# Head norms: sums on four 32-column groups, and factors spread by one fp32r matmul per head from a rounded row and a remainder row

## What is computed

```python
def rms_norm(x, g):
    y = xf * lax.rsqrt(jnp.mean(xf * xf, axis=-1, keepdims=True) + EPS)
    return (y * g).astype(x.dtype)

h = rms_norm(from_chunks(h), norm_g.reshape(ML_HEADS, ML_DH))   # 4 heads of 192
o = rms_norm(from_chunks(o), norm_g.reshape(HG_HEADS, HG_DV))   # 6 heads of 128
qd = rms_norm_2(q_d.reshape(B, S, DIL_HEADS, DIL_DIM), g_q_dil) # 8 heads of 128
kd = rms_norm_2(k_d.reshape(B, S, DIL_HEADS, DIL_DIM), g_k_dil)
q_nope, k_nope = rms_norm_2(q_nope, g_q_nope), rms_norm_2(k_nope, g_k_nope)
```

## Time and profile before

| | us |
|---|---|
| median of 3 runs | 2983.12 (2980.38 to 2985.36) |
| span of the profiled execution | 2978.0 |
| PE busy | 2946.2 (99%) |
| DVE busy | 2051.0 (69%) |
| ACT busy | 1311.7 (44%) |
| DMA | 50.7% of 16 engines, 178 GB/s |

### The profile page before, as it was taken

The page is one execution under the profiler, slowest core; times in us unless marked ns, Lnnn a source line. Parts: engine busy times, 40 slices in busy tenths (PEclk is TensorE's granted clock), DMA queues, the critical chain, the costliest instruction groups (busy, mean ns, idle before and its releaser), DMA issues.

```text
span 2978.0 us, 47097 instructions
## 1 busy us (share of the span) xinstructions
PE 2946.2 (99%) x18616; PEld 2630.0 (88%) x18616; DVE 2051.0 (69%) x2624; ACT 1311.7 (44%) x1418; POOL 70.0 (2%) x72
## 2 busy tenths in 40 slices
PE   8999999999999999999999999999999999999999
PEld 8898898999988888888888888876998888888888
DVE  6675787977788888885557776636666666666444
ACT  5354423444444444444444354425445444444333
POOL 0000000000001000000000000000000000000000
PEclk9999999999999999999999999999999999999999
DMA  6553334555555555555555544531555555555555
GB/s 230 184 183 134 114 120 149 168 173 198 186 196 193 189 196 194 190 182 190 193 195 198 195 172 168 186 122 43 184 198 186 195 197 188 193 197 177 194 193 184
DMA packets 87359, 530.39 MB, mean 178 GB/s; under 512 B 9952, under 2 KB 10336, under 8 KB 41184
## 3 DMA queue, kind: packets, MB, share of 16 engines
q1 hardware_dynamic: 87264, 529.07, 50.7%
HBM read 526.94 MB, written 2.10 MB: 178 GB/s over the span
## 4 chain that ended last, share of the span: by engine, by line
PE 96%; DVE 2%; ACT 1%; DMA 0%; issue 0%; SPq 0%; DVEq 0%; ACTq 0%
PE bank L576 74%; PE late L576 22%; DVE arena L1687 1%; DVE w_low L1687 0%; DVE half_low L1687 0%; DVE arena L1684 0%; ACT w_high L1203 0%; PE late L1144 0%; DVE arena L1989 0%; DMA ring<-in_w_gates 0%; DMA xT<-in_xT 0%; DVE acts_both L1687 0%; DVE arena L2045 0%; DVE arena L2016 0%; DVE xrs L1734 0%
## 5 line engine op out<-in xcount | busy, mean ns | idle before, releaser
L1687 DVE TENSOR_TENSOR w_low<-ring,w_high 128x2048 fp32r<-128x2048 f32 (+1 forms) x480 | 1014.3, 2113 | 384.1 <-ACT w_high L1203 380.2
L1203 ACT ACTIVATE w_high<-ring 128x2048 fp32r<-128x2048 f32 (+1 forms) x480 | 849.5, 1771 | 636.0 <-DMA ring<-in_w_down 223.0
L576 PE MATMUL bank<-up_early,w_high 128*128 128x512 f32 x1408 | 487.8, 389 | 0.0
L576 PE MATMUL bank<-up_late,w_high 128*128 128x512 f32 x1408 | 487.3, 389 | 0.0
L576 PE MATMUL late<-acts_both,w_high 128*128 128x512 f32 x1408 | 479.0, 389 | 0.3 <-DVE w_low L1687 0.3
L576 PE MATMUL bank<-up_early,w_low 128*128 128x256 f32 x1408 | 388.6, 276 | 0.0
L576 PE MATMUL late<-acts_both,w_low 128*128 128x256 f32 x1408 | 388.6, 276 | 0.0
L576 PE MATMUL bank<-up_late,w_low 128*128 128x256 f32 x1408 | 388.6, 276 | 0.0
L576 PEld LDWEIGHTS bank<-up_early,w_high 128*128 128x128 f32 x1408 | 264.5, 188 | 55.2
L576 PEld LDWEIGHTS late<-acts_both,w_high 128*128 128x128 f32 x1408 | 264.3, 188 | 55.1 <-DVE w_low L1687 0.6
L576 PEld LDWEIGHTS bank<-up_late,w_high 128*128 128x128 f32 x1408 | 264.0, 188 | 54.7
(11 more groups left out here) (311 smaller groups left out, 4946.2 us busy)
## 6 DMA issues: line engine op xcount, KB each, us to landing
ring<-in_w_up SPq DMA_DIRECT2D x176, 1024.0 KB, 4.7
ring<-in_w_down SPq DMA_DIRECT2D x128, 704.0 KB, 4.0
ring<-in_w_in SPq DMA_DIRECT2D x66, 1024.0 KB, 4.7
ring<-in_w_mix SPq DMA_DIRECT2D x62, 1024.0 KB, 4.8
ring<-in_w_gates SPq DMA_DIRECT2D x96, 512.0 KB, 3.7
ring<-in_w_branch SPq DMA_DIRECT2D x16, 1024.0 KB, 4.7
ring<-in_w_out SPq DMA_DIRECT2D x16, 1024.0 KB, 4.8
ring<-in_w_o SPq DMA_DIRECT2D x16, 1024.0 KB, 4.8
```

Source lines behind the costliest of these rows:

```text
L576: return nc.tensor.matmul(o, lhsT, rhs, start=first, stop=last)
L1203: A(w_high[:, s, 0:cols], ring[:, s, 0:cols], ACT.Copy).then_inc(rounded[s], 1)
L1687: return V.tensor_tensor(o, a, b, op)
```

## The change

It alters the two matmul steps of a head norm and the DVE step between them. No matmul is added or removed.

- **Sums.** `pick` windows are 32 columns wide instead of 8, and head h goes to output partitions 32*(h%4) on, so four heads in a row use four different 32-column groups of the array. The order is piece by piece, heads inside. The ones stand twice in a window, so that a head's sum lies in row 32*(h%4) + h//4 and again 16 rows lower.
- **Factors.** DVE works on all 128 partitions. Its last step becomes three: the product rounded to fp32r into `rows_r`, the exact product into `xms`, and `rows_r * sign + xms`, where `sign` is 0 in the upper 16 rows of a group and -1 in the lower 16. The upper rows so hold the rounded factor, the lower the remainder.
- **Spread.** The stationary operand is a column of `row_sel` (fp32r) with ones in the two rows of a head; it and `rows_r` are fp32r, so each matmul adds rounded factor and remainder in one pass.
- **Set-up.** `pick` grows from 45 to 108 columns, ACT copies 128 x 8 values into `row_sel` once, TensorE waits for that (`sel_made`), and `rows_r` lies over the end of `s5p`.

```diff
-            return pick[:, part, HEADS - 1 - h:2 * HEADS - 1 - h]
+            c = ROW_PICK * part + 1 - h // 4
+            return pick[:, c:c + 32]
@@ sum_squares
-                    parts = [x for parts in n["groups"] for x in parts]
-                    for k, (one, sq) in enumerate(parts):
-                        last = mm(bank[4][0:HEADS, 0], one, sq, k == 0, k == len(parts) - 1)
+                    heads, pieces = len(n["groups"]), len(n["groups"][0])
+                    for k in range(pieces):
+                        for h in range(heads):
+                            one, sq = n["groups"][h][k]
+                            q = 32 * (h % 4)
+                            last = mm(bank[4][q:q + 32, 0], one, sq, k == 0 and h < 4,
+                                      k == pieces - 1 and h >= heads - 4)
@@ spread_rows
+                pe.wait_ge(sel_made, 1)
                 for h in range(rows_):
-                    last = mm(bank[4 + h // 2][:, h % 2], spread(h, P), xrs[:])
+                    last = mm(bank[4 + h // 2][:, h % 2], row_sel[:, h:h + 1].broadcast_to([P, P]), rows_r[:])
@@ scalar engine
+            act.wait_ge(cst_landed, 48)
+            A(row_sel[:], row_where, ACT.Copy).then_inc(sel_made, 1)
             act.wait_ge(conv_ready, 1)
@@ vector engine
+            def rows_out():
+                rs, tmp = xrs[:], xtmp[:]
+                link(V.reciprocal(rs, rs))
+                link(tt(tmp, xms[:], rs))
+                link(tt(tmp, tmp, rs))
+                link(V.tensor_scalar(tmp, tmp, -0.5, 1.5, M, ADD))
+                tt(rows_r[:], rs, tmp)
+                link(tt(xms[:], rs, tmp))
+                stt(rows_r[:], rows_r[:].bitcast(F32), row_sign, xms[:], M, ADD).then_inc(norm_rows, 1)
...
-                ms, rs, tmp = xms[0:n["rows"]], xrs[0:n["rows"]], xtmp[0:n["rows"]]
-                V.tensor_scalar(ms, bank[4][0:n["rows"], 0], 1.0 / n["n"], EPS, M, ADD).then_inc(norm_mean, 1)
+                V.tensor_scalar(xms[:], bank[4][:, 0], 1.0 / n["n"], EPS, M, ADD).then_inc(norm_mean, 1)
```

More of the change, by code:

```diff
@@ L64 @@
 HEADS = 8
+ROW_PICK = 33
 SLOPES = [2.0 ** -(h + 1) for h in range(HEADS)]
@@ L223, in build @@
         cst = sb("cst", [P, 3, P])
-        pick = sb("pick", [P, 3, 2 * HEADS - 1])
+        pick = sb("pick", [P, 3 * ROW_PICK + 1 + HEADS])
+        row_sign, row_where = pick[:, 3 * ROW_PICK:3 * ROW_PICK + 1], pick[:, 3 * ROW_PICK + 1:]
+        row_sel = ctx.enter_context(nc.sbuf_tensor("row_sel", [P, HEADS], R32))
         w_if = sb("w_if", [P, KT, 32 + ML])
@@ L232, in build @@
         s5p = sb("s5p", [P, S5_STEPS, 2, S5_STATES])
+        rows_r = nc.alloc_sbuf_tensor_at("rows_r", [P, T], R32, offset=nc.sbuf_base - S5_STEPS * 2 * S5_STATES * 4)
         small = sb("small", [P, 2, 8])
@@ L349, in build @@
         norm_rows, norm_spread = sem("norm_rows_ready"), sem("norm_rows_spread")
+        sel_made = sem("row_selection_made")
         conv_ready, conv_act, qk_ready = sem("ml_conv_ready"), sem("ml_conv_act"), sem("ml_qk_ready")
@@ L1301, in root @@
                 if "rows" in n:
-                    m, r = xms[0:n["rows"]], xrs[0:n["rows"]]
+                    m, r = xms[:], xrs[:]
                 else:
@@ L1730, in row_factors @@
                 dve.wait_ge(norm_summed, norm[0])
-                ms, rs, tmp = xms[0:n["rows"]], xrs[0:n["rows"]], xtmp[0:n["rows"]]
-                V.tensor_scalar(ms, bank[4][0:n["rows"], 0], 1.0 / n["n"], EPS, M, ADD).then_inc(norm_mean, 1)
+                V.tensor_scalar(xms[:], bank[4][:, 0], 1.0 / n["n"], EPS, M, ADD).then_inc(norm_mean, 1)
                 dve.wait_ge(norm_rooted, norm[0])
[L1734 to L1738, removed]
+                rows_out()
             def factor(h):
@@ L2404, in mean_step @@
                 if "rows" in n:
-                    last = V.tensor_scalar(xms[0:n["rows"]], bank[4][0:n["rows"], 0], 1.0 / n["n"], EPS, M, ADD)
+                    last = V.tensor_scalar(xms[:], bank[4][:, 0], 1.0 / n["n"], EPS, M, ADD)
                 elif len(n["groups"]) == 1:
@@ L2418, in root_step @@
                     return n["rs"]
[L2419 to L2423, removed]
                 casts[0] += 1
-                tt(rs, rs, tmp).then_inc(norm_rows, 1)
+                rows_out()
                 dve.wait_ge(norm_rows, casts[0])
@@ L2740, in host_layout @@
     a["cst"] = cst
[L2741 to L2745, removed]
+    pick = np.zeros((P, 3, ROW_PICK), np.float32)
+    for c in (1, 17):
+        pick[:, 0, c] = 1
+        pick[:, 1, c] = i < 64
+        pick[:, 2, c] = i >= 64
+    sign = -(i % 32 >= 16).astype(np.float32)[:, None]
+    h = np.arange(HEADS)[None]
+    where = (i[:, None] // 32 == h % 4) & (i[:, None] % 16 == h // 4)
+    a["pick"] = np.concatenate([pick.reshape(P, -1), sign, where.astype(np.float32)], axis=1)
     hm = np.zeros((P, 8, P), np.int32)
```

## The result

| | before | after |
|---|---|---|
| median, us | 2983.12 (7 runs, 2974.51 to 2985.36) | 2993.59 (7 runs, 2990.64 to 2995.43) |
| span of the profiled execution | 2978.0 | 2993.6 |
| ratio | | 1.0046 [1.0035, 1.0058] |

What follows compares the result with a forecast made beforehand. TensorE bounds the kernel, busy 2946.2 of 2978.0 us with 96% of the chain. 9.6 + 9.2 + 3.6 - 0.9 - 0.7 = 20.8 us off gives 2957.2, with 5.1 around it 2962.3 us; range 2955 to 2972.

Steps and rivals of the forecast that it cites:

- Sums and spreads: The norms' two matmul steps: eight sums in 1.07 us instead of 3.62, eight spreads in 1.12 instead of 3.62.
- The first rival: Sums on the column groups run one after the other: a gain of only 8.9 us, 2974.2 us; chance 0.06.
- the partial overlap: Column groups of the sums overlap only partly: two rounds take 1.12 us instead of 0.86, 2963.6 us; no chance given.
- the new drains: Edges of the sums: twelve tiling-mode drains of 0.1 to 0.2 us would be new, 1 to 2 us.
- QD and KD: Two head norms: sums 2 x 2.55 and spreads 2 x 2.50 less 0.5 of waiting, 9.6 us gained together.
- QN and KN: Two head norms ahead of attention: DVE and TensorE arrive together, 9.2 us gained of 10.1 removed.
- ML and HG: Two head norms: at ML DVE carries the chain, 0.9 us lost; at HG sums and spread on chain, 3.6 gained.
- Clock: Behind ML: one more half-clock stretch, costing 1.5 us, about as likely as not; half put in, 0.7 us lost.
- The rival that the clock stays low: Attention, from 2019 us on, at clock 0.50: 25 to 27 us lost against 20.8 gained, 2987 us; chance 0.02.
- the change's set-up: ACT's copy into the new tile and the load of the longer `pick`: nothing; uncovered they would cost 0.2 us.
- 5.1 us around the span: Outside the profiled span: the runs' median lies 5.1 us above it (2983.1 against 2978.0), taken as unchanged.

Runs made afterwards that it cites:

- seventh experiment: Changed kernel with `pick` and `row_sel` behind the arena and every other tile at its place in the kernel before: 2954.58 us, 0.9922.
- the tenth: Kernel before with 288 unused bytes behind `ones`, so `ones` and the gate weights keep their places: 2980.92 us, 1.0011.
- the sixth: Kernel before with 288 unused bytes behind `pick`, so each tile behind it lies where the changed kernel has it: 3018.92 us, 1.0147.
- the fourteenth: Changed kernel with all small tiles 384 bytes and the arena 512 bytes behind their places in the kernel before: 2994.08 us, 1.0040.
- the first experiment: Kernel before with the arena alone 256 bytes higher: 2976.48 us, 0.9999.
- the twelfth: Kernel before with `ones` alone moved behind the arena, 32 bytes past a multiple of 128: 3017.19 us, 1.0134.
- the eleventh: Changed kernel with `ones` alone moved behind the arena, to a multiple of 128 bytes: 2958.46 us, 0.9931.

## Why the prediction was wrong

**The terms of the sum held.** The seventh experiment is the change alone, with nothing moved, and is what I had costed: 2976.22 to 2954.58, 21.6 us less (by the interval 18 to 28), where the forecast had 20.8. That the totals agree so closely is in part luck, since misses in the points below cancel. Point by point, in its trace:

- *Sums and spreads.* 1.07 us where I had 1.07, and 1.23 with the tail where I had 1.12. The first rival (groups one after the other) falls; so does the partial overlap, and the new drains that the Trainium skill's "TensorEngine Tiling (Array Packing)", Key Properties, would have made of twelve edges: the first pair starts 1.00 us behind the sums (1789.60 and 1790.60 in the changed kernel), which is two rounds of 0.43 and 0.14 for the edge; before, eight sums in a row took 3.5 us to that point, 0.43 each and 0.1 for the edge.
- *QD and KD.* From QD's sums to the pair behind KD's spread: 66.0 us in the seventh (1770.99 to 1837.01), 75.1 before: 9.1 gained, 9.6 forecast. The wait ahead of KD's spread is 0.22 us, 0.35 forecast.
- *QN and KN.* The transposes of the earlier trace rows start at 1997.70, 21.5 us earlier; 8.1 of it falls here, 9.2 forecast. Behind KD's spread 158 pairs ran in rhythm 350, which cost 1.6; in the changed kernel they don't, and the gain up to the transposes is 9.7. The place given in the prediction was 1998.4.
- *ML and HG.* TensorE's wait for `half_low` ends 0.9 us later against the sums, as forecast (383.61 in the changed kernel, with sums that start 0.5 later). HG, from its sums to the branches behind it, brought 3.2 in the seventh and 3.9 in the changed kernel; 3.6 forecast. The same stretch differs by 0.9 us between two traces without the change (210.8 before, 209.9 in the tenth).
- *Clock.* I had put in 0.7 lost. The changed kernel has two stretches at half clock at ML (length, busy (records), granted clock, DMA share, GB/s) where the earlier trace rows has one, but the first lies where DVE carries the chain:

```profile
366.90:373.70 6.80, 6.02 (x28) 0.50 0.05 20
...
384.00:387.40 3.40, 3.40 (x18) 0.50 0.24 76
```

In exchange this stretch of the kernel before, in attention, is missing:

```profile
2021.10:2027.90 6.80, 6.80 (x17) 0.50 0.14 59
```

Those are 17 records in 6.8 us at 1.2 GHz. But they come and go without the change: two of the nine traces without it have such a stretch in attention, and four of the seven with it. From the first transpose to the output projection it takes 150.0 us in the kernel before and in the seventh, which have such a stretch, and 147.0 in the changed kernel and in the tenth, which have none; and the tenth has the instructions of the kernel before, with other room between its tiles:

```profile
2018.34 0.63 PE L1145 MATMUL late<-cst,arena 128*128 128x128 f32 x4 [1.18 <-DVE arena L1685]
...
2165.30 0.39 PE L577 MATMUL bank<-out_both,w_high 128*128 128x512 f32 x1
```

So 3.0 of the 12.8 us that QN, KN and attention brought in the changed kernel are the clock's chance, and 3.0 of the 2978.0 that I started from are too. At ML the stretch behind 382 us is missing in the seventh, and from the resumed `gate()` to HG's sums it takes 75.5 us where it took 77.05: 1.5 less. So where I had put in 0.7 lost, the clock gave back 1.5 in the seventh and 3.0 in the changed kernel; neither changes a verdict. The rival that the clock stays low falls.

**The step that failed** is one that the prediction didn't write down as a term: that stages whose code the change doesn't touch take the time they took. I looked at the change's set-up ("`pick` is 63 columns longer and is loaded among the first constants ... Both nothing") and priced its load and its copy. What those 63 columns and `row_sel` move was in the diff, 288 bytes for everything allocated behind them, and I gave it no line. Its price by the ledger is 40.6 us, by experiment 3018.92 - 2976.22 = 42.7 us in the sixth, and 3017.19 - 2977.70 = 39.5 us for `ones` alone. The prediction put it at nothing without a reason. The chance of 0.02 for slower went to a mechanism that did not happen, and the true one had none.

A smaller mistake: I put 5.1 us around the span, from the median of three runs. The profiled run itself took 2980.38 us for a span of 2978.0; in the changed kernel 1.8 us lie around it. That term was 3 us too large.

Two rules of the Trainium skill stand beside this. "TensorE: Matmul & The Clock Gate", Back-to-back issue gap, gives an isolated gap of N / 2.4 + 2.5 ns: 215.8 ns for 512 columns and 109.2 for 256, an estimate of 325 ns a pair; it has no term for the operands' addresses. The section adds that in a stream with weight loads the formula counts too much at large N; here it counts too little, since this trace has 340 or 350. And "SBUF — State Buffer", Operand start alignment, asks for multiples of the element size and says that this is about legality, not speed, and that its runs timed nothing; all places here are multiples of 32 and legal, and they differ by up to 1.5% of the kernel.

**What stays open.** Why `ones` at 160 past a multiple of 256 leaves rhythm 350 behind it and at 128 rhythm 340; at 0, in the fourteenth, it gives 350 in both up stages and 340 in the in projections. The traces show durations that differ by a few ns, no stall that they name. Whether 256 is the period, whether the measure is `ones` alone or its place against the other operands (`hT`, the weight ring and the arena begin at 128 too), and what makes 192 a matter of chance, isn't settled. Nor is it known what starts rhythm 350 at the output projection (2161.18 in the changed kernel, and in the first experiment), where nothing is idle ahead of it, or why the arena at a multiple of 256 makes the first block shorter and the later stages longer. It wasn't tried whether a short wait put in behind the matmul with `ones` would bring rhythm 340 back.

## To carry to other kernels

A change that adds or widens an on-chip tile moves every tile allocated behind it: compare the addresses before and after, and time the old kernel with the new layout (one unused tile) beside the new kernel, so that the edit and the move are told apart. If stages that were not edited change their length in a trace, read the starts of consecutive matmuls there, since a change of 10 ns in 340 is seen in no busy share. Here the edit was worth keeping with its new tiles put behind the last big one: 2954.58 us, 0.9922 of before.

## What the runs showed of the hardware

- Pairs of fp32r matmuls (512 and 256 columns, each with its own load of 128 columns) run at 0.34 or 0.35 us a pair at the same granted clock of 1.00 (2.4 GHz). They keep to one for hundreds of us (350 from 2161 to 2990 us in the changed kernel), and change mostly at interruptions: a float32 matmul (855.10 in the twelfth), idle time of 0.33 us (1332.74 in the eleventh, from 340 to 350; with 0.34 at 1336.73 in the kernel before they stay at 340), or of 0.11 us (1348.09 in the changed kernel, from 350 to 340).
- Which one follows behind the float32 matmul with `ones` depends on where that stationary tile lies (340 at 18 of 18 places with 128 past a multiple of 256, 350 at 15 of 15 with 160): moved by 32 bytes, that tile alone made the kernel 1.3% slower.
- With the arena 384 bytes further (it holds the moving operand of half the pairs of an up stage and of all of a down stage, and `w_high` for all), those pairs came every 0.347 us: 7 us more for an up stage, 4.5 to 4.7 for a down stage, while the work ahead of the first output projection took 9.1 us less.
- A stretch of 6.8 us at half clock in attention costs 3.0 us (150.0 against 147.0 us), and is there or not in traces of the same instructions (there before, missing in the tenth).
- Four float32 matmuls on different 32-column groups of the array, all writing one bank, take the time of one: 16 records in 1.07 us, where eight on 8 columns took 3.62.
